# Loading the combined log-and-exponential table set on ScalarE ahead of the down projections

## The reference, cut to what matters

```
x += 0.5 * post1(SwiGLU_1(pre1(x)))
x += post2(W_out concat[A, B, C, D](pre2(x)))
x += 0.5 * post3(SwiGLU_2(pre3(x)))
```

```
def rms_norm(x, g):
    xf = x.astype(jnp.float32)
    y = xf * lax.rsqrt(jnp.mean(xf * xf, axis=-1, keepdims=True) + NORM_EPS)
    return (y * g.astype(jnp.float32)).astype(x.dtype)
```

```
logf = jax.nn.log_sigmoid(fb.astype(jnp.float32) + fox_b.astype(jnp.float32))
g = -jnp.exp(a_log.astype(jnp.float32)) * jax.nn.softplus(ac.astype(jnp.float32) + dt_bias.astype(jnp.float32))
beta = jax.nn.sigmoid(bc.astype(jnp.float32))
```

## Time and profile before

| what | us |
|---|---|
| median of 3 runs | 1596.89 |
| the 3 runs | 1596.89, 1599.01, 1589.54 |
| the profiled execution, its own time | 1584.76 |
| its span, first to last instruction | 1583.0 |
| TensorE busy in the span | 1337.1 |
| VectorE busy | 921.3 |
| ScalarE busy | 676.7 |

### The profile page before, as it was taken

How to read it: one execution, slowest core, us unless ns; L and a number is a source line. 1 busy time by engine, 2 the same in 40 slices (tenths; PEclk the granted TensorE clock), 3 DMA queues, 4 the chain that set the end, 5 groups by cost and what they waited for, 6 DMA issues and landing times.

```text
span 1583.0 us, 27964 instructions
## 1 busy us (share of the span) xinstructions
PE 1337.1 (84%) x9968; PEld 1247.4 (79%) x9968; DVE 921.3 (58%) x1496; ACT 676.7 (43%) x1085; POOL 217.3 (14%) x176
## 2 busy tenths in 40 slices
PE   5999979977586579999979999798966757699997
PEld 5999979965474379999979999698754636599996
DVE  4666355485655655664466654555766554566633
ACT  4664454234200365554455644444250013565543
POOL 1000011023332230000110000200333331200000
PEclk9999989967787589999989999899577967899998
DMA  6565563354462234555645645453545513255553
GB/s 214 169 190 160 162 198 107 122 158 124 147 182 79 82 119 133 182 180 146 187 133 173 198 144 167 143 172 99 148 151 166 155 42 109 81 183 185 161 173 92
DMA packets 286118, 234.15 MB, mean 148 GB/s; under 512 B 19898, under 2 KB 282018, under 8 KB 286056
## 3 DMA queue, kind: packets, MB, share of 16 engines
q1 hardware_dynamic: 286056, 233.37, 48.5%
HBM read 228.65 MB, written 5.37 MB: 148 GB/s over the span
## 4 chain that ended last, share of the span: by engine, by line
PE 75%; DVE 16%; ACT 4%; issue 4%; DMA 1%; SPq 1%; POOL 0%; DVEq 0%; ACTq 0%; POOLq 0%
PE ps L1398 19%; PE ps L1399 19%; PE ps L1400 19%; PE ps L1597 2%; PE ps L1695 2%; DVE s L1121 2%; DVE nlo L944 2%; PE ps L1542 1%; PE ps L1694 1%; DVE yt L927 1%; PE ps L1545 1%; PE ps L1511 1%; PE ps L1685 1%; ACT whi L592 1%; PE ps L1740 1%
## 5 line engine op out<-in xcount | busy, mean ns | idle before, releaser
L1398 PE MATMUL ps<-nhi,whi 128*128 128x264 f32 x1936 | 564.6, 292 | 64.9 <-DVE nlo L944 42.2
L897 DVE TENSOR_TENSOR wlo<-raw,whi 128x1024 fp32r<-128x1024 f32 (+2 forms) x376 | 394.7, 1091 | 283.5 <-ACT whi L592 283.2
L1399 PE MATMUL ps<-nlo,whi 128*128 128x264 f32 x1936 | 559.1, 289 | 0.0
L1400 PE MATMUL ps<-nhi,wlo 128*128 128x264 f32 x1936 | 558.2, 288 | 0.0
L1398 PEld LDWEIGHTS ps<-nhi,whi 128*128 128x128 f32 x1936 | 375.9, 194 | 71.6 <-DVE nlo L944 33.0
L592 ACT ACTIVATE whi<-raw 128x1024 fp32r<-128x1024 f32 (+2 forms) x376 | 336.5, 945 | 181.9 <-PE ps L1400 110.1
L1399 PEld LDWEIGHTS ps<-nlo,whi 128*128 128x128 f32 x1936 | 375.9, 194 | 0.2
L1400 PEld LDWEIGHTS ps<-nhi,wlo 128*128 128x128 f32 x1936 | 373.8, 193 | 0.0
L1398 PE MATMUL ps<-hhi,whi 128*128 128x264 f32 x704 | 202.2, 287 | 9.1 <-DVE hlo L914 9.1
L1400 PE MATMUL ps<-hhi,wlo 128*128 128x264 f32 x704 | 201.4, 286 | 0.0
L1399 PE MATMUL ps<-hlo,whi 128*128 128x264 f32 x704 | 201.1, 286 | 0.0
(11 more groups left out here) (340 smaller groups left out, 1526.5 us busy)
## 6 DMA issues: line engine op xcount, KB each, us to landing
raw<-in_ffn_gate_dram SPq DMA_DIRECT2D x44, 1024.0 KB, 5.3
raw<-in_ffn_up_dram SPq DMA_DIRECT2D x44, 1024.0 KB, 5.4
raw<-in_ffn_down_dram SPq DMA_DIRECT2D x64, 704.0 KB, 4.5
raw<-in_w_in_dram SPq DMA_DIRECT2D x24, 1024.0 KB, 5.7
kslot<-in_cache_fox_k_dram SPq DMA_DIRECT2D x128, 128.0 KB, 2.7
vslot<-in_cache_fox_v_dram SPq DMA_DIRECT2D x128, 128.0 KB, 2.4
raw<-in_w_out_dram SPq DMA_DIRECT2D x8, 1024.0 KB, 5.0
kslot<-in_state_swa_k_dram SPq DMA_DIRECT2D x32, 128.0 KB, 2.6
```

Of the source, the lines that this page charges most:

```text
L897: tt2(wlo[s][:, a:b], raw[s][:, a:b], whi[s][:, a:b].bitcast(F32), ALU.subtract).then_inc(S(f"w_lo{s}"), 1)
L1398: mm(out, wh, hi_, start=first, stop=False)
L1399: mm(out, wh, lo_, start=False, stop=False)
L1400: return mm(out, wl, hi_, start=False, stop=last)
```

## The change

load_table now asks for a set by its name, natural_log_exp_and_others, which holds both the logarithm and the exponential, in place of running Ln once, which brought in the logarithm's own set. The tile spare goes. Nothing else is edited; behind its deletion every line number is one lower.

```diff
-        spare = place("spare", [P, 1])
...
                     def load_table():
 
-                        act.activation(spare[:, :], C("eps"), ACT.Ln)
+                        act.preload_act_table_set("natural_log_exp_and_others")
```

## The result

The changed kernel takes 1573.31 us (median of 4, 1572.86 to 1573.84) against 1593.22 us for the kernel before (median of 4, 1588.06 to 1599.01). The ratio is 0.988, 95% interval 0.9843 to 0.9917: faster by 1.2%, by more than the 0.6% that I forecast. The time lies in the stated range, at its low edge, 10 us under the predicted 1583. The profiled executions stand closer together: 1584.76 us before, 1572.86 after, 11.9 us apart, where the sum was 10.1 and its upper bound 11.

The account below looks back on a forecast made before the run. TensorE was taken as the bound, busy 84% of the span, with ScalarE on the chain only at norms between phases. 5.2 + 3.9 + 1.0 = 10.1 us off 1593.2 gave 1583, range 1573 to 1594.

Parts of the forecast that it names:

- the sum: Whole kernel: 5.2 at post norms, 3.9 at pre norms, 1.0 for TensorE's clock; 10.1 us gained, from 6.5 to 11.
- Where the loads lie: Fourteen loads go; those of the exponential at four post and three pre norms count, the others gain nothing.
- 1.30 us each: Exponential's load at four post and three pre norms: each gains 1.30 us; post norms kept at 0.8 to 1.30.
- The hidden places: Logarithm's loads at three pre norms and four loads at the gates: worth 0 us, the gates between 0 and 0.2.
- the cover by TensorE's first pair: At pre norms, TensorE's first pair of slots hides the logarithm's load; ScalarE idles some 3.4 us behind it; gain nothing.
- the gates: Four loads at the gates of the mixers: 0 us, between 0 and 0.2; the copy of cum stays where it was.
- the weights landed in time at the boundary: Norm 0 of layer 1: next weights land by about 811.3, are split at 812.3 afterwards, leaving 1 us of cover.
- The clock, 1.0 us: Behind norm 0 of layer 1: with idle time 1.33 instead of 2.63 us, TensorE's clock stays full; 1.0 us, 0 to 1.7.
- The drain: Table switches: the skill page adds 1.38 us of drain to the 1.28 load; the trace leaves no room for it.
- From the profile to the median: Whole kernel: the 10.1 us gain was taken from 1593.2, the middle of four executions, giving 1583 for the new median.
- rival 3: Mixers begin in another rhythm, TensorE's clock does not rise: up to 13 us a layer, net +16, 1609; chance 3%.
- My own signs of being wrong: First product after a pre norm waits for a DMA, mixers' clock differs from 0.76, or time falls over 16 us.

Follow-up runs that it names:

- norm 0's load alone: Changed kernel with one load put back between logarithm and exponential of norm 0 in layer 1; 1581.08 us, ratio to before 0.9952.
- the post norms alone: Changed kernel with the logarithm's own set loaded again ahead of norm 2 (both layers) and norm 0 (layer 1); 1585.43 us, ratio to before 0.9986.
- the hidden loads: Changed kernel with seven combined-set loads back, ahead of the logarithm at three pre norms and at the gates; 1573.27 us, ratio to before 0.9906.

## Why the prediction was right, and where it was off

- **Where the loads lie.** Right. Seven on the path, seven hidden, shown by putting back either set: 0 us for the hidden seven, the whole gain for the others.
- **1.30 us each.** Right for six (1.26 to 1.29). Norm 5 of layer 0 gave 0.79, just under the lower bound of 0.8: I had taken VectorE to be idle for the whole load at every post norm and not read how long; there it was 0.69 us, and low parts for the next layer were queued ahead. The 5.2 of the post norms was 4.6.
- **The hidden places, the cover by TensorE's first pair, the gates, the weights landed in time at the boundary.** Right as far as the profiles show. At the gates the copy of cum stands 6.77 us behind their start without the loads, and 6.76 with them put back.
- **The clock, 1.0 us.** Near in size for the fall that I meant: both falls together are 1.8 us, and the one at the start of dn1 alone is 0.96, which leaves 0.8. The reason was wrong. The step that failed: after an idle time of 1.65 us the clock stayed and after 2.63 it fell, so I expected no fall after 1.33. In the runs with norm 0's load alone and with the post norms alone the idle time was 2.63 us and the clock stayed; 2.38 us ahead of dn1 made it fall in one kernel and not in the other. So the length of the stop does not decide by itself. That the moment decides with it fits all the rows and was not tested by itself.
- **The drain.** The Trainium skill, "ScalarE: Activation LUTs", section "What ACT_TABLE_LOAD costs", has 2.66 us for a switch. Six real switches that went gave 1.26 to 1.29 us each. This agrees with the rows of before and not with the page.
- **From the profile to the median.** This failed, and it is the bulk of the 10 us by which 1583 was too high. I took the spread of the kernel before as noise that the changed kernel would share. It was no noise in the two long executions with a profile: it was rival 3's mechanism, the mixers' clock, at work in the kernel before. How many of its executions it takes is not known; two of its five profiles show it. The change moved the mixers' start away from the edge, as far as two profiles and ten executions within 2.7 us tell. Rival 3 had price and place nearly right (up to 13 us a layer; measured 3.8 to 12.5) and the side wrong: the sum put the mixers' clock at nothing, and even between the two profiles it gave 1.4 us. The evidence that I held against it, equal readings in both layers of one profile, was that of one short execution.
- **The sum.** Against the profiled execution: 1574.7 forecast, 1572.86 measured. The gain of 11.9 lies above the stated 6.5 to 11, and those bounds are not quite what the terms give: 4 x 0.8 + 2.9 + 0 = 6.1 and 5.2 + 3.9 + 1.7 = 10.8.
- **My own signs of being wrong.** Two of the three came up. The clock in the stretch behind the gates reads 0.73 in both layers and not 0.76, and the time fell by 19.9 us between the medians, over 16 (against the larger number of executions of before it is 14.5). A gain over 1% had 11% in the forecast, of which the larger part was a lucky draw. So the time came out inside the range partly by luck: the range was wide enough for a gain that the sum did not hold.

What stays open: why the mixers take just these times for each moment of the fall (1.74 us is harmless, 1.26 and 2.32 cost over 10), and how the executions of the changed kernel would lie in a larger number; it was timed 4 times, and 6 more with the hidden loads in. That a kernel with TensorE kept busy in the mixers would lose the spread was not tried.

## What to carry to other kernels

For a function that alternates between two table sets, look first for a set that holds both, and ask for it by name where ScalarE idles; then judge each load that goes by who waited for it, and read how long that one waited. Before a few us are forecast, time the old kernel often: if its executions spread by more than the change is worth, find out what spreads them: here a delay of 1.3 us cost 7.8 us in the median. Compare profiles stage by stage, not spans, and time the kernels that are to be compared side by side.

## What the runs showed that I had not expected

- The mixers of one and the same kernel take 251.2 or 255.1 or 261.8 us, and which of them goes with 0.1 to 0.2 us in when TensorE's clock falls at the gates (1.14: 251.4, 1.26: 261.8, 1.29: 255.0).
- In the medians one load of 1.3 us cost 7.4 us at norm 1 of layer 0 and 7.8 us at norm 0 of layer 1; two loads at the first place cost 3.0 (by the ratios some 5, 7 and 1).
- In two pairs of profiles the clock's fall in layer 1 comes at much the same moment (0.64 and 0.73 in the changed kernel and with the hidden loads; 3.99 and 4.00 with one and two loads at norm 1 of layer 0), though in layer 0 it lies far apart (3.55 and 0.93; 2.63 and 1.21). Four other variants have the fall of layer 1 at 1.05, 1.40, 3.62 and 3.68. What ties the pairs together was not tested.
